# The first expert block of each layer picked by TensorE from SBUF instead of by an indirect DMA

## The reference, cut to what matters

```python
x = x + g1 * mixer(modulate(rms_norm(x), ...))
hl = modulate(rms_norm(x), sh2, sc2)              # "h2": what the router and the experts read
scores = sigmoid(h @ router_w)                    # 16 per token; best group of 4, best two experts in it
gates = one_hot(exp_idx) weighted by w / sum(w)
for e in range(16):                               # FF = 512
    a = silu(h @ w_gate[e]) * (h @ w_up[e])
    y = y + gates[:, e:e+1] * (a @ w_down[e])
x = x + g2 * y
```

## Time and profile before

| | us |
|---|---|
| median of three runs (lowest, highest) | 1166.86 (1164.23, 1170.43) |
| profiled execution, first to last instruction | 1166.4 |
| PE busy in it | 983.8 (84%) |
| DVE busy | 402.4 (34%) |
| ACT busy | 365.3 (31%) |
| POOL busy | 218.6 (19%) |

### The profile page before, as it was taken

How to read it: one execution, slowest core, us unless ns; L and a number is a source line. 1 busy time by engine, 2 the same in 40 slices (tenths; PEclk the granted TensorE clock), 3 DMA queues, 4 the chain that set the end, 5 groups by cost and what they waited for, 6 DMA issues and landing times.

```text
span 1166.4 us, 24481 instructions
## 1 busy us (share of the span) xinstructions
PE 983.8 (84%) x9634; PEld 662.7 (57%) x9635; DVE 402.4 (34%) x848; ACT 365.3 (31%) x777; POOL 218.6 (19%) x329
## 2 busy tenths in 40 slices
PE   4899999988899979799898659999999768996571
PEld 1577777544555655466566447887555644664340
DVE  1533331346733522122122283122853621221113
ACT  3532222466832222122222344233751211120101
POOL 0000000000000034244344201910000132442221
PEclk9899999999999999899999879999999898998895
DMA  9766655998230759999999467224527789999983
GB/s 338 276 225 223 224 214 175 338 362 324 112 137 36 251 205 396 422 422 422 422 425 393 168 226 174 75 72 138 224 83 308 301 355 419 404 421 425 424 358 115
DMA packets 92967, 321.76 MB, mean 276 GB/s; under 512 B 21289, under 2 KB 33234, under 8 KB 80610
## 3 DMA queue, kind: packets, MB, share of 16 engines
q1 hardware_dynamic: 85026, 305.00, 67.9%
q0 software_dynamic: 7008, 12.62, 2.9%
q10 hardware_dynamic: 864, 3.15, 0.7%
HBM read 313.28 MB, written 13.99 MB: 281 GB/s over the span
## 4 chain that ended last, share of the span: by engine, by line
PE 66%; DMA 18%; DVE 6%; issue 4%; ACT 3%; SPq 1%; POOL 1%; POOLq 0%; DVEq 0%; ACTq 0%
PE ps L1953 22%; PE ps L1719 21%; DMA expert_sets<-in_moe_w_up_dram 10%; PE ps L1874 7%; PE ps L1616 5%; PE ps L1640 4%; DMA expert_sets<-in_moe_w_down_dram 3%; DMA ring<-in_ada_w_dram 2%; PE ps L1774 1%; PE ps L1801 1%; DMA ada_late<-in_ada_w_dram 1%; PE ps L1830 1%; DMA expert_rows<-moe,scatter_idx 1%; DMA val<-expert_rows 1%; PE ps L1657 1%
## 5 line engine op out<-in xcount | busy, mean ns | idle before, releaser
L1953 PE MATMUL ps<-expert_sets,moe 128*32 128x256 f32 x6304 | 366.7, 392 | 79.3 <-DMA expert_sets<-in_moe_w_up_dram 37.0
L1953 PEld LDWEIGHTS ps<-expert_sets,moe 128*32 128x32 f32 x6304 | 241.4, 113 | 203.3 <-issue 97.2
L1543 DVE STREAM_TRANSPOSE moe<-moe 128x256 f32<-128x256 f32 x70 | 45.8, 654 | 313.9 <-PE ps L1953 284.2
L1719 PE MATMUL ps<-w_high,x_high 128*128 128x512 f32 x352 | 142.0, 404 | 6.5 <-DVE x_low L490 5.1
L1719 PE MATMUL ps<-w_low,x_high 128*128 128x512 f32 x352 | 138.6, 394 | 0.0
L1719 PE MATMUL ps<-w_high,x_low 128*128 128x512 f32 x352 | 138.5, 393 | 0.0
L1092 ACT ACTIVATE moe<-ps 128x128 f32<-128x128 f32 x68 | 18.9, 278 | 318.5 <-PE ps L1953 309.4
L477 DVE TENSOR_TENSOR w_low<-ring,w_high 128x2048 fp32r<-128x2048 f32 x24 | 55.5, 2321 | 134.7 <-ACT w_high L474 134.7
L760 POOL MEMSET moe<- 128x128 f32 x2 | 0.4, 205 | 539.3 <-PE ps L1900 539.3
L784 POOL DMA_INDIRECT expert_rows<-moe,scatter_idx x74 | 76.0, 1027 | 85.6 <-POOL scatter_idx L821 41.4
L1719 PEld LDWEIGHTS ps<-w_high,x_high 128*128 128x128 f32 x352 | 66.7, 189 | 30.3 <-issue 14.7
(11 more groups left out here) (245 smaller groups left out, 1089.5 us busy)
## 6 DMA issues: line engine op xcount, KB each, us to landing
expert_sets<-in_moe_w_down_dram SPq DMA_DIRECT2D x32, 2048.0 KB
expert_sets<-in_moe_w_gate_dram SPq DMA_DIRECT2D x30, 2048.0 KB
expert_sets<-in_moe_w_up_dram SPq DMA_DIRECT2D x30, 2048.0 KB
ring<-in_ada_w_dram SPq DMA_DIRECT2D x16, 2048.0 KB, 8.1
ring<-in_diff_w_qkv_dram SPq DMA_DIRECT2D x6, 2048.0 KB, 8.7
ada_late<-in_ada_w_dram SPq DMA_DIRECT2D x6, 2048.0 KB, 12.4
ring<-in_na_w_qkv_dram SPq DMA_DIRECT2D x6, 2048.0 KB, 8.7
val<-expert_rows SPq DMA_DIRECT2D x12, 512.0 KB, 4.6
```

The source lines that it names most:

```text
L1543: dve.transpose(blk_inT, blk_in[b].rearrange("p (j k) -> p k j", k=KC)).then_inc(m_xt[l], 1)
L1719: mm = pe.matmul(ps[:, n % 2], x_part[:, k, tok], w_part, start=(k == 0 and i == 0), stop=(k == KC - 1 and i == 2))
L1953: mm = pe.matmul(ps[g * SLOTS:(g + 1) * SLOTS, bank, 0:n_out], lhs_T[:, k, :], weights(k, g), start=(k == 0), stop=(k == n_chunks - 1), sk ...
```

## The change

Block 0 is no longer gathered from HBM. After the ranks are known, DVE makes marks that say which token of each row of 128 has rank s in expert 0, for s = 0 to 31 (two instructions). PE multiplies the h2 rows in SBUF with these marks: for each of 8 column groups and each row of 128 tokens a 128x128 stationary operand and 32 moving columns. The stationary operand takes every eighth number of the row. ACT copies the 128x256 result to `blk_inT`. Gathers begin with block 1; block 2's follows at once. The dummy scatters are gone, and the first one or two rounds of the block loops are written out, without a wait for a scatter. The copy of layer 0's last turned row goes to `hT` instead of to the place of the first h2 row, so that all h2 rows stay. SP waits for the picking matmuls before it loads the third expert's down matrix over the h2 rows.

```diff
 # DVE, routing, behind the wait for the ranks
+                of_first = rt[:, 15, 0:nt]
+                step(stt(of_first, r3(10)[:, :, 0], -float(NOT_IN_FIRST), ps[:, 4, 0:w].rearrange("p (a b) -> p a b", b=N_EXP)[:, :, 0],
+                         ALU.mult, ALU.add))
+                stt(first_marks[:, 0:nt], const("slot").unsqueeze(1).to_broadcast([P, nt, SLOTS]), -float(NOT_IN_FIRST),
+                    of_first.unsqueeze(2).to_broadcast([P, nt, SLOTS]), ALU.add, ALU.is_equal).then_inc(s_mk, 1)
 # PE, behind the ranks (before: keep_busy 9 or 7, slot table, keep_busy 11 or 10, gates_ups)
+                def gather_first():
+
+                    pe.wait_ge(s_h[l], nt)
+                    pe.wait_ge(s_mk, l + 1)
+                    for k in range(KC):
+                        for m, t in enumerate(TILES_OF[l]):
+                            mm = pe.matmul(ps[:, 5, k * SLOTS:(k + 1) * SLOTS], heads_out(l, t).rearrange("p (d k) -> p k d", k=KC)[:, k],
+                                           first_marks[:, m], start=(m == 0), stop=(m == nt - 1))
+                    mm.then_inc(s_g1, 1)
...
                 pe.sem_inc(m_dn[l], 1)
+                keep_busy(2)
+                gather_first()
                 gates_loaded(0)
-                gates_ups(0, 0)
+                if l == 0:
+                    slot_table()
+                gates_ups(0, 0, first=True)
+                if l == 1:
+                    slot_table()
+                keep_busy((6, 26)[l])
                 pe.wait_ge(s_idx[l], 2)
 # ACT
                 for m in range(2):
                     keep(m)
+                act.wait_ge(s_g1, l + 1)
+                act.copy(blk_inT, ps[:, 5, 0:DG].rearrange("p (k s) -> p k s", s=SLOTS)).then_inc(m_xt[l], 1)
                 act.wait_ge(s_idx[l], 2)
 # SP
                 sp.wait_ge(s_lg[l], NT[l] + 1)
+                sp.wait_ge(s_g1, l + 1)
                 expert_weights(l, 2, 2, 2)
 # POOL
-                for b in range(2):
-                    gather(b, slot_idx[:, b:b + 1])
-                pool.memset(blk_none, 0.0).then_inc(m_ix[l], 1)
-                pool.wait_ge(m_ix[l], 2)
-                pool.tensor_copy(scatter_idx[:, 1:2], ...)
-                pool.tensor_copy(scatter_idx[:, 0:1], ...)
-                pool.wait_ge(m_ix[l], 4)
+                gather(1, slot_idx[:, 1:2])
+                gather(0, slot_idx[:, 2:3])
                 pool.wait_ge(s_idx[l], 2)
                 pairs = pool.value_load(...)
-                scatter(1, blk_none)
-                pool.wait_ge(m_sc[l][1], 16)
-                for b in range(2):
-                    scatter(b, blk_none)
-                for b in range(2):
-                    (wait m_xt b + 1, copy the index of block b + 2, gather(b))
+                (wait m_xt 2, copy the index of block 3, gather(1))
 # DVE, blocks
-                dve.wait_ge(m_ga[l][0], 16)
-                turn_block_in(0)
```

More of the change, by code:

```diff
@@ L217, in turned_row @@
         def turned_row(l, m):
[L219 removed]
+            if l == 0 and m == TILES - 1:
+                return hT[:, :, 0:P]
+            return ao[:, m + 1 if l == 0 else 2 + m].rearrange("p (k t) -> p k t", t=P)
         LATENT_ROWS, GAIN_ROW = (2, 3, 4, 0), 1
@@ L798, in _, with block_in_and_out @@
                 in_turn()
-                scatter(1, blk_none)
-                pool.wait_ge(m_sc[l][1], 16)
-                for b in range(2):
-                    scatter(b, blk_none)
-                for b in range(2):
[L804 to L809, removed]
+                pool.wait_ge(m_xt[l], 2)
+                pool.tensor_copy(gather_idx[:, 1:2], slot_idx[:, 3:4]).then_inc(m_ix[l], 1)
+                pool.wait_ge(m_ix[l], 2)
+                in_turn()
+                gather(1)
+                def block_in_and_out(j):
                     for b in range(2):
@@ L1094, in _ @@
                             act.wait_ge(m_dn[0], 2 * j + b + 1)
-                            act.wait_ge(m_sc[0][1 - b], 16 * j + 16)
+                            if not (isinstance(j, int) and j < 2 - b):
+                                act.wait_ge(m_sc[0][1 - b], 16 * j - 16 * (1 - b))
                             copy_block_out(blk_out[1 - b])
+                alone = (2, 0)[l]
+                for j in range(alone):
+                    block_act(j)
+                with act.Fori(alone, pairs) as j:
+                    block_act(j)
                 if l == 0:
@@ L1561, in _ @@
                         if l == 1:
-                            dve.wait_ge(m_sc[1][1 - b], 16 * j + 16)
+                            if not (isinstance(j, int) and j < 2 - b):
+                                dve.wait_ge(m_sc[1][1 - b], 16 * j - 16 * (1 - b))
                             tt(blk_out[1 - b], ps[:, 5, 0:DG], gate_tile, ALU.mult).then_inc(m_y[1], 1)
+                alone = (0, 2)[l]
+                for j in range(alone):
+                    block_steps(j)
+                with dve.Fori(alone, pairs) as j:
+                    block_steps(j)
                 if l == 1:
@@ L1937, in _, with slot_table @@
                 mm.then_inc(s_rk[l], 1)
[L1939 to L1946, removed]
+                def gather_first():
[6 more added lines that the diff above has]
+                    mm.then_inc(s_g1, 1)
+                def slot_table():
+                    pe.wait_ge(s_oh[l], 2)
+                    for q in range(2 * nt):
+                        for g in range(GROUPS):
+                            mm = pe.matmul(ps[g * SLOTS:(g + 1) * SLOTS, 4, P:P + BLK_COLS], oh_slot[:, q], oh_blk[:, q],
+                                           start=(q == 0), stop=(q == 2 * nt - 1), skip_group_check=True)
+                    mm.then_inc(s_tab[l], 1)
                 def block_products(bank, n_out, lhs_T, n_chunks, weights):
@@ L1955, in block_products, with gates_ups @@
                     return mm
-                def gates_ups(i, which):
+                def gates_ups(i, which, first=False):
                     pe.wait_ge(m_xt[l], i + 1)
-                    pe.wait_ge(m_ac[l], i + 1)
+                    if not first:
+                        pe.wait_ge(m_ac[l], i + 1)
                     block_products(0, 2 * FG, blk_inT, KC, lambda k, g: gate_and_up(which, k, g)).then_inc(m_gu[l], 1)
```

39 lines of the change are left out of this document (21 added, 18 removed).

## The result

The changed kernel takes 1174.49 us (median of 4 runs, 1172.19 to 1177.15), beside 1165.55 us for the kernel before on the same chip: a ratio of 1.0075, 95% interval 1.0045 to 1.0105. It is slower, where 1155 (1149 to 1163) was forecast. Its profiled execution took 1172.58 us, its span 1170.3 us.

A forecast was written before the change was run, and what follows sets the result against it. The prediction took the chain of waits before the expert-weight stream starts, with PE releasing later loads, as the bound. Gains of 7.0 (layer 0) and 4.8 (layer 1), 11.8 off 1166.4, gave 1154.6, so 1155 us; range 1149 to 1163.

The forecast's parts named there:

- 32 x 0.133 = 4.3: Layer 0's picking on PE: 32 matmuls at 0.133 us each take 4.3 us, ending at 411.0.
- my 2.1: Layer 1's picking on PE: 16 x 0.133 = 2.1 us, ending at 917.1.
- my timing of block 1: Layer 1: block 1's gather is there at about 931.0 and PE starts the block at 932.0, against 936.50 before.
- The bound of 0.30: Upper bound for one strided picking matmul, 0.30 us: a 192 ns weight load stretched 1.57 times, with nothing overlapping.
- rival B: Picking ahead of the slot table on PE delays later blocks' indices; at 0.5 a matmul, time 1172; chance 0.06.
- Rival A: The strided stationary operand costs about twice, 0.24 a matmul, 7.7 and 3.8 us of picking; time 1160.5; chance 0.22.
- The mechanism behind the sum: Both layers: a gain is worth what it moves the weight stream's start, if PE moves as much; 7.0 + 4.8 us.
- the hole that I had reckoned at 1.6: Layer 1's weight stream: empty at 945.2, next load at 946.8 after block 1's downs, a hole of 1.6 us.
- of the two shifts the smaller counts: Gain is the smaller of the stream's and PE's shifts; layer 1 had 5.3 and 4.6, taken as 4.8 us.
- I expect full clock: Layer 0's first blocks at granted clock 1.00; block 2's gates and ups take 3.7 instead of 5.4 us.
- The 1.03 of "issue": Layer 0: an inner-loop step of 1.03 us between blocks 1 and 2, so block 2 starts at 426.1.
- A cost put at nothing: Layer 0: SP's down load of the third expert waits for picking, to 411.1; cost 0.

The follow-up runs named there:

- e1_contiguous: The changed kernel with each picking matmul's stationary operand 128 contiguous numbers of the h2 row instead of every eighth (wrong column order); 1163.3 us, ratio to before 0.9980.
- e6_half: The changed kernel with only four of the eight column groups picked, leaving out half of block 0's input; 1167.0 us, ratio to before 1.0002.
- e9_swap_short_busy: The changed kernel with picking's operands swapped (marks stationary, h2 rows moving) and 12 instead of 26 `keep_busy` calls in layer 1; 1158.7 us, ratio to before 0.9927.
- e3_table_first: The changed kernel with the slot table ahead of picking on PE in both layers, no `keep_busy` behind block 0's gates; 1176.8 us, ratio to before 1.0098.
- e2_swapped: The changed kernel with picking's operands swapped, slot table ahead of block 0's gates in both layers, and `keep_busy` moved and shortened; 1152.1 us, ratio to before 0.9876.
- e4_no_dummies: The changed kernel without picking: block 0 gathered as before, dummy scatters gone, first loop rounds written out; 1161.2 us, ratio to before 0.9961.

## Why the prediction was wrong

**The step that failed: "Picking: 8 x 4 = 32 matmuls", "32 x 0.133 = 4.3".** It measured 15.37, off in both factors. The count: a float32 matmul of the source is two pairs of instructions (weight load and matmul) in the profile, and I priced by rows that count instructions. The rows said so: the earlier trace rows has x8 for the ranks' four matmuls of the source and x64 for the slot table's 32. It is 64, which adds 32 x 0.133 = 4.3. The price: 0.240 in place of 0.133, another 64 x 0.107 = 6.8, of which the step is 5.8 and the rest what the contiguous pairs of e1_contiguous cost over 0.133, with the clock down for a part of them. In layer 1 it is 2.1 + 32 x 0.109 = 5.6 over my 2.1. The same slip missed the 26 `keep_busy` of layer 1: 52 instructions and 11.49 us, of which my timing of block 1 had nothing. With my other times they would have ended near 933.3 (an estimate, 921.8 + 11.49) and not let block 1 start at 932.0.

**The bound of 0.30** held for an instruction, 0.240; the number I multiplied was the wrong one. By the matmul of the source it is 0.48, and what I called rival B at 0.5 came out nearly line by line: picking ends at 421.8 (422.7), the gather leaves at 424.94 (425.3), block 1 starts at 432.07 (431 to 433), 3.9 lost in layer 0 (5) and 0.5 in layer 1 (0), 1172.6 for the profiled execution (1172). It had a chance of 0.06, and hitting the time so closely is partly luck, since the median is 1174.5. Rival A, 0.24 an operand, was the right price of an instruction with the wrong count; e6_half plays it and gives 1167.0 where A said 1160.5. I put that down to the clock and to layer 1's `keep_busy`, which A took as free; no run separates the two.

**The mechanism behind the sum was right for layer 0.** I argued that a gain is worth what it moves the start of the stream. In the fourteen kernels of the table, layer 0's stage less the offset of its first stream load is 225.7 to 227.2, while the offset runs from 32.8 to 48.6. In layer 1 it is 212.1 to 214.6 in eight and 217.2 to 218.9 in six. The six had their second gate load 20.6 us or more behind the first, seven of the eight 16.3 to 18.7 (e9_swap_short_busy 21.3): the hole that I had reckoned at 1.6 grows when PE's block 1 lags, so "of the two shifts the smaller counts" is borne out roughly, not exactly.

**Rival B's mechanism was half right.** It named the slot table behind picking, and the chain of the changed kernel runs as it said: picking, slot table, gather. But e3_table_first frees the table and is no faster, since block 0, which needs the picking itself, then holds block 1.

**Clock.** "I expect full clock" failed in the stretch of the picking: 0.50 from 415 to 425 (with picking short, in e2_swapped, it stayed at 1.00), which made the slot table 1.56 and not 0.92, block 0's gates 4.61 and not 3.66. After block 1's start it was 1.00, as forecast, and 0.68 before.

**Small ones.** The 1.03 of "issue" between blocks 1 and 2 didn't come: L1985 runs x327 from 432.07 without a break, so the estimate was too slow by 1 there. In layer 1 a gap is there once PE is early (2.11 in e2_swapped, 2.49 forecast). The dummy scatters' removal was worth more than I gave it: e4_no_dummies gained 5.2 in layer 0 where the sum had 2.9.

**A cost put at nothing.** SP's down load moved from 404.59 to 421.89, 3 us ahead of block 1's gather, and that gather then took 6.2 from its issue to DVE's transpose (424.94 to 431.12), not my 4.6. It took 5.4 to 6.4 in the six kernels with long picking in this order, and 3.3 to 4.6 in before, e4_no_dummies and four of the five swapped ones (e9_swap_short_busy 5.3). So up to 1.6 of layer 0's loss may be this load, as rival A had named it; no run moves the load alone.

## What to carry to other kernels

Multiply a price by the count that the profile gives for a row of the same kind, not by the loops of the source: the x of the row against the source's count is the first thing to check. When a selection matrix is narrow, make it the stationary operand and let the wide rows move, contiguous; read at a step of 16 or 32 bytes as the stationary operand, in float32, they cost double here at full clock. And a filler before a wait is a wait itself: when a step ahead of it is moved, its length has to be set anew.

## What was unexpected of the hardware

- A float32 weight load of 128x128: 192 ns contiguous, 196 at step 2, 329 at step 4, 335 at step 8 with the clock granted in full; 333, 331, 330 and 335 at half clock.
- The granted clock fell to 0.50 while PE was 100% busy, with picking instructions of 32 moving columns (from 411 us in the changed kernel, and in e1_contiguous and both other steps too). Being busy didn't keep the clock.
- An instruction with 32 stationary and 256 moving columns took 0.06 us (1.94 / 32) at full clock, a quarter of the 0.24 of one with 128 strided stationary and 32 moving, and there were half as many.
